# Attention of the sample sequences: GpSimd issues the odd fills, ScalarE copies the odd chunks of turned keys

## What is computed

```python
def gathered_attention(q, t, kg, vg, s, tbl):
    logits = jnp.einsum('bqgrd,bqgnd->bqgrn', q, kg, ...) * (q.shape[-1] ** -0.5)
    ...
    p = masked_softmax(logits + ..., ...)
    return jnp.einsum('bqgrn,bqgnd->bqgrd', p.astype(vg.dtype), vg)
...
o_slc = gathered_attention(qa, t, gather_rows(c_slc_k, page_table, ks, s, g_a), gather_rows(c_slc_v, page_table, vs, s, g_a), s, tbl_a)
o_win, _ = dense_attention(qa, t, k_w, v_w, s_w, tbl_a, WINDOW)
o_b = gathered_attention(qb, t, k_b, v_b, s_b, tbl_b)
```

## Time and profile before

| | us |
|---|---|
| median of 3 runs | 3385.72 |
| lowest and highest of them | 3378.32 and 3390.58 |
| the profiled execution's own time | 3371.94 |
| its span | 3370.3 |
| TensorE busy in the span | 2977.2 (88%) |
| VectorE busy | 1373.4 (41%) |
| ScalarE busy | 708.3 (21%) |
| GpSimd busy | 108.4 (3%) |

### The profile page before, as it was taken

How to read it: one execution, slowest core, us unless ns; L and a number is a source line. 1 busy time by engine, 2 the same in 40 slices (tenths; PEclk the granted TensorE clock), 3 DMA queues, 4 the chain that set the end, 5 groups by cost and what they waited for, 6 DMA issues and landing times. The chain is left out here.

```text
span 3370.3 us, 56792 instructions
## 1 busy us (share of the span) xinstructions
PE 2977.2 (88%) x22144; PEld 2631.9 (78%) x22144; DVE 1373.4 (41%) x2245; ACT 708.3 (21%) x1084; POOL 108.4 (3%) x150
## 2 busy tenths in 40 slices
PE   6799999999975889897887775599799999999897
PEld 3599999999963478786553554499699999999897
DVE  2322222212214368465741666633533343333433
ACT  2211111211102021120000443321322222222222
POOL 0000000000000000000000112100000000000000
PEclk8799999999987899897986887799899999999998
DMA  9765676777544732333897223343233333334331
GB/s 342 229 188 168 196 219 209 224 220 218 172 130 125 209 117 61 108 100 96 276 303 248 79 95 129 111 131 87 66 95 104 94 93 92 104 93 114 108 89 51
DMA packets 594867, 496.75 MB, mean 147 GB/s; under 512 B 37148, under 2 KB 515885, under 8 KB 593885
## 3 DMA queue, kind: packets, MB, share of 16 engines
q1 hardware_dynamic: 528408, 408.45, 41.3%
q10 hardware_dynamic: 58496, 60.59, 5.5%
q0 software_dynamic: 7840, 26.10, 2.0%
HBM read 460.02 MB, written 48.70 MB: 151 GB/s over the span
## 5 line engine op out<-in xcount | busy, mean ns | idle before, releaser
L146 PE MATMUL psum<-h_high,w_high 128*128 128x260 f32 x4992 | 1009.3, 283 | 21.6 <-DVE w_low L133 21.6
L146 PE MATMUL psum<-h_high,w_low 128*128 128x260 f32 x4992 | 1006.9, 283 | 0.0
L146 PE MATMUL psum<-h_low,w_high 128*128 128x260 f32 x4992 | 1005.2, 283 | 0.0
L146 PEld LDWEIGHTS psum<-h_high,w_high 128*128 128x128 f32 x4992 | 770.5, 189 | 35.9 <-issue 30.1
L146 PEld LDWEIGHTS psum<-h_high,w_low 128*128 128x128 f32 x4992 | 770.7, 189 | 0.0
L146 PEld LDWEIGHTS psum<-h_low,w_high 128*128 128x128 f32 x4992 | 768.9, 189 | 0.0
L133 DVE TENSOR_TENSOR w_low<-w,w_high 128x2048 fp32r<-128x2048 f32 x162 | 370.9, 2291 | 591.6 <-ACT w_high L128 591.6
L128 ACT ACTIVATE w_high<-w 128x2048 fp32r<-128x2048 f32 x162 | 309.2, 1910 | 479.5 <-PE psum L146 361.3
L609 DVE COPY pj_out<-psum 128x260 f32<-128x260 f32 x66 | 28.3, 429 | 429.8 <-PE psum L146 429.8
L567 ACT ACTIVATE pj_out<-psum 128x260 f32<-128x260 f32 x66 | 25.6, 388 | 593.9 <-PE psum L146 593.9
L199 PE MATMUL psum<-w,c 128*32 128x512 f32 x768 | 105.3, 661 | 26.1 <-DMA w<-in_w_ada 17.5
(11 more groups left out here) (374 smaller groups left out, 2829.2 us busy)
## 6 DMA issues: line engine op xcount, KB each, us to landing
w<-in_w_ada SPq DMA_DIRECT2D x96, 1024.0 KB, 8.1
w<-in_w_in_att SPq DMA_DIRECT2D x65, 1024.0 KB, 11.7
w<-in_w_in_conv SPq DMA_DIRECT2D x64, 1024.0 KB, 6.3
proj<-pj_out POOLq DMA_DIRECT2D x66, 260.0 KB, 5.0
cz_pgk<-in_cache_nsa_cmp_k SPq DMA_DIRECT2D x128, 128.0 KB, 2.1
cz_pgv<-in_cache_nsa_cmp_v SPq DMA_DIRECT2D x128, 128.0 KB, 2.2
w<-in_w_out_att SPq DMA_DIRECT2D x16, 1024.0 KB, 6.4
w<-in_w_out_conv SPq DMA_DIRECT2D x16, 1024.0 KB, 6.3
```

Of the source, the lines that this page charges most:

```text
L146: mm = pe.matmul(k.psum[:, banks + hf, 0:HC], w[:, kt, :], x[:, kt, hf * HC:(hf + 1) * HC], start=(kt == 0 and m == 0), stop=(kt == KT - 1 ...
```

## The change

SP keeps the even fills. The odd fills go from ScalarE to GpSimd, which issues fills 1, 3, 5 and 7 ahead of its memsets and the others behind them. The copies of turned keys are split by the chunk's number: VectorE copies the even chunks (bank 3), ScalarE the odd ones (bank 4), and the one semaphore `kept` becomes two, `kept_v` and `kept_a`. ScalarE's exponentials now stand between its copies. The odd slots' arrival semaphores are allocated once for the program instead of in the stage.

```diff
+    arrived = [k.at_filled[b // 2] if b % 2 else k.sem(f"at_arrived{b}") for b in range(SLOTS)]
...
+        def keep_keys(eng, kind, s):
+            tb, u, odd = INFO[kind][1] // 2, KINDS.index(kind) * NS + s, int(eng is nc.scalar)
+            if u >= 2:
+                eng.wait_ge(used, u - 1)
+            for c in range(odd, tb, 2):
+                q = chunk0[kind] + s * tb + c
+                to, turned_keys = kt[:, s % 2, :, c * 256:(c + 1) * 256], ps[:, 3 + q % 2, :].rearrange("p (g q) -> p g q", g=G)
+                eng.wait_ge(turned, q + 1)
+                if odd:
+                    eng.activation(to, turned_keys, ACT.Copy).then_inc(kept_a, 1)
+                else:
+                    eng.tensor_copy(to, turned_keys).then_inc(kept_v, 1)
...
             @block.gpsimd
             def _(pool):
+                for n in range(1, SLOTS, 2):
+                    fill(pool, n)
                 pool.memset(pns[:, :, :], 0.0).then_inc(padded, 1)
                 pool.memset(pts_all[:, :, :, :], 0.0).then_inc(padded, 1)
                 pool.memset(pts_win[:, :, :, :], 0.0).then_inc(padded, 1)
                 pool.wait_ge(padded, 3)
+                for n in range(SLOTS + 1, len(fills), 2):
+                    fill(pool, n)
...
-                            pe.wait_ge(kept, q - 1)
+                            pe.wait_ge(kept_a if q % 2 else kept_v, q // 2)
...
-                    pe.wait_ge(kept, chunk0[kind] + (s + 1) * (npg // 2))
+                    for kept in (kept_a, kept_v):
+                        pe.wait_ge(kept, (chunk0[kind] + (s + 1) * (npg // 2)) // 2)
...
-                after = {fill_of["dsa", 0, 5] + 6: "slc", fill_of["slc", 1, 3] + 6: "dsa", fill_of["dsa", 1, 3] + 6: "win"}
-                for n in range(1, len(fills), 2):
-                    fill(act, n)
...
+                for s in range(NS):
+                    keep_keys(act, "slc", s)
+                for s in range(NS):
+                    keep_keys(act, "dsa", s)
+                    if s == 2:
+                        exponentials("slc")
+                exponentials("dsa")
+                for s in range(NS):
+                    keep_keys(act, "win", s)
+                exponentials("win")
```

More of the change, by code:

```diff
@@ L1209, in stage_attend_samples @@
             "dsa": (1, PG, "cache_dsa_k", "cache_dsa_v", KB, "dsa_v_s", None)}
-    vnew_in, turned, kept, used, padded, vused, o_kept, o_turned, added = (
-        k.sem("at_" + n) for n in ("vnew", "turned", "kept", "used", "padded", "vused", "o_kept", "o_turned", "added"))
+    vnew_in, turned, kept_a, kept_v, used, padded, vused, o_kept, o_turned, added = (
+        k.sem("at_" + n) for n in ("vnew", "turned", "kept_a", "kept_v", "used", "padded", "vused", "o_kept", "o_turned", "added"))
     top, maxed, top_all, shifted, topped, exped, summed, sum_all, rated, prob, diag, pt_mm, placed = (
@@ L1217, in stage_attend_samples @@
     SLOTS = 8
-    arrived = [k.sem(f"at_arrived{b}") for b in range(SLOTS)]
+    arrived = [k.at_filled[b // 2] if b % 2 else k.sem(f"at_arrived{b}") for b in range(SLOTS)]
     fills = [(kind, kv, f) for kind, kv in PHASES for f in range(NS * INFO[kind][1] // 8)]
@@ L1517, in exponentials @@
                         nc.scalar.activation(pn[:, i, sh:sh + 1], ps[0:32, MISC[kind], sh:sh + 1], ACT.Exp, bias=st[0:32, i, 1, sh:sh + 1]).then_inc(exped[kind], 1)
-                after = {fill_of["dsa", 0, 5] + 6: "slc", fill_of["slc", 1, 3] + 6: "dsa", fill_of["dsa", 1, 3] + 6: "win"}
-                for n in range(1, len(fills), 2):
-                    fill(act, n)
[L1523 to L1530, removed]
+                act.wait_ge(cs_step, 3)
+                nc.scalar.activation(cs_p[:, 0, :], ps[0:NS * NH, 3, 0:NCB], ACT.Exp, bias=cs_st[:, 1:2], accum_out=cs_st[:, 2:3]).then_inc(cs_exp, 1)
+                act.wait_ge(cs_out, 1)
+                nc.scalar.activation(cs_pt[:, :], ps[:, 3, 0:NS * NH], ACT.Copy).then_inc(cs_kept, 1)
+                for s in range(NS):
[8 more added lines that the diff above has]
+                exponentials("win")
             @block.vector
@@ L1573, in compressed @@
                         dve.tensor_copy(cols(k.oS[:, 0, :]), cols(ps[:, 4 - g, 256:256 + R])).then_inc(cs_step, 1)
[L1575 to L1583, removed]
                 def own_tops(kind):
@@ L1670, in _ @@
                 for s in range(NS):
-                    keep_keys("slc", s)
+                    keep_keys(dve, "slc", s)
                 for s in range(NS):
-                    keep_keys("dsa", s)
+                    keep_keys(dve, "dsa", s)
                     if s == 0:
@@ L1689, in _ @@
                 for s in range(NS):
-                    keep_keys("win", s)
+                    keep_keys(dve, "win", s)
                 keep_outs("dsa", "win")
@@ L2436, in build @@
         k.y_out = [k.sem(f"y_out{b}") for b in range(2)]
+        k.at_filled = [k.sem(f"at_filled{b}") for b in range(4)]
         k.w_in = [k.sem(f"w_in{s}") for s in range(4)]
```

## The result

The changed kernel takes 3388.17 us (median of 12 runs, 3382.39 to 3391.50) against 3380.19 us of the kernel before on the same chip (12 runs, 3374.29 to 3390.58). The ratio is 1.0021, with a 95% interval of 1.0012 to 1.0031: slower by 4 to 10 us. That lies inside the 0.3% that the forecast called no change and is still a loss that can be measured; the forecast had no term for it. The profiled execution took 3385.51 us, its span is 3383.8.

A forecast was written before the change was run, and what follows sets the result against it. Key part bound by the copy-transpose ring, coinciding with VectorE's limit; value part by transfers. Terms sum to -0.3 us on 3371.94, so 3371.6; the runs' median lies 13.8 higher, hence 3385. Own range 3377 to 3395; 8-in-10 range 3374 to 3425.

The forecast's parts named there:

- Ring: Key part: copy and transposes take turns on each PSUM bank, 1.44 us a pair; splitting copies gains only at sequence starts, -1 us.
- GpSimd's issue: Page fills: GpSimd issues 264 more DMAs at 0.67 us each, a fill in 5.9 us; it fits barely, adding 0.
- the first rival: Page fills: GpSimd's issue is serial or slower in a row; stage ends 35 to 114 us later; chance 0.24.
- Exponentials: Key part: an odd key copy on ScalarE waits behind exponentials until 1681.89, once; +0.7 us.
- ScalarE's lost issues: Page fills: ScalarE no longer issues the odd fills; its queue waited for slots, so this is worth nothing.
- Moved memsets: Stage start: GpSimd's memsets end at about 1599, the value part needs them after 1720; no effect.
- Half the bytes on another queue: Value part: odd fills move to GpSimd's queue, no difference in cost per byte taken; 0, ends 6 us either way.
- The sum: Changed stage: all terms together, -1 + 0.7 + 0 + 0 = -0.3 us, on the profiled execution's 3371.94.

## Why the prediction was wrong, point by point

- **Ring, right.** Pairs turn in 1.45 us. ScalarE's copy is 0.597 us, not 0.69, and shortens only its own bank. A sequence gained 0.17 us where under 0.1 was forecast; the key part gained 1.4 us (115.8 against the mean of 116.8 and 117.7), for -1 forecast.
- **GpSimd's issue, right.** 0.58 us for 0.67 taken, with pauses of 2.7 and 3.0 us between fills in the key part: no wait for GpSimd's issue was added, and the first rival, with a chance of 0.24, fell. A pace of 1 us is not to be seen.
- **Exponentials, +0.7: too much.** The odd copy behind them starts at 1679.00 in the changed kernel, 1.17 us behind the even one instead of the usual 0.43, as forecast; but that sequence takes 7.68 us instead of 7.33, so +0.35 reaches TensorE's pace. ScalarE's lost issues, 0: no run told them apart from the ring.
- **Moved memsets, "Nothing": wrong.** I asked what waits for the memsets and not what stands beside them. The lead got 1.8 us shorter (29.6 against 31.4), half of what a second profile of before varies by itself.
- **"Half the bytes on another queue": the step that failed.** The forecast put this term at 0, with ends of 6 us either way for what a byte costs on each queue; that cost stayed (347 GB/s against 348). The value part measured +6.5 us, and from which fill gets the bytes first: SyncE's fill 66 came 6.5 us later into the part, behind GpSimd's 67. The forecast's held the clue, as the packets are larger on one queue: 26.10 MB in 7840 packets against 60.59 MB in 58496.
- **No term for other stages.** The sum ended with the changed stage. That put the second prompt stage at nothing without a reason; it lost 6.1 us, through the stores that GpSimd issues there. The Trainium skill, "SBUF — State Buffer", section "Who interferes with whom", describes ports that GpSimd shares with VectorE in its two-port modes: whoever issues first has them for the whole instruction, and the other stands still. The 2.14 us, which end behind GpSimd's instruction, agree; the 0.52 us in the same order before do not.
- **The sum.** Between the first profiles, lead, key part, value part and prompt 2 give -1.8 - 0.9 + 6.5 + 6.1 = +9.9 us, inside the measured 4 to 10; these executions lie 13.5 us apart, 4.0 of them in the first prompt stage, which varies by as much in kernels with no fill on GpSimd. That the forecast's 3385 came within 3 us of 3388.17 is luck: it stands on three runs of before with a median of 3385.72, and twelve have 3380.19. On that scale the forecast is 3380.

## What to carry to other kernels

Where two queues feed one consumer in turn, equal total rate is not enough: compare the bytes per packet and the order in which fills land, and look for the last wait that everything behind it hangs on. Queues with equal packets kept the order here; a hold on one of them mended 3.7 of 6.5 us. Before work is put beside GpSimd or taken from there, list VectorE's instructions with both ends in SBUF in every stage that GpSimd issues or computes in: here some stood still for up to 1.6 us beside a store and 4.4 us beside memsets. And when a measured loss is larger than the changed stage's, cut both traces at the same landmarks before looking for a cause.

## What the runs showed of the hardware

- In some stretches two queues got equal counts of packets (553 and 551, 1330 and 1310), so bytes went there by packet size: 78% to GpSimd's packets of 3.4 KB on average. From 1800 to 1807 us the counts were 526 and 1095, and GpSimd's queue still got 59% of the bytes.
- The same 1 KB rows went in packets of 4096 bytes when GpSimd issued the fill and of 1024 bytes when SyncE or ScalarE did.
- GpSimd's transfers in a row are issued every 0.58 us.
- VectorE's 128x512 product in SBUF, started 0.30 us into GpSimd's issue of a store, took 0.52, 1.25, 1.24 and 2.12 us with 74 to 79 transfers issued by GpSimd before, and 2.12 to 2.15 us as soon as 8 more had gone ahead, some 500 us earlier. Why 8 transfers matter so long after was not found. The long ones end 0.28 us behind GpSimd's next instruction.
- Two table copies of 32x64 took 4.69 us beside GpSimd's memsets and 0.28 us alone.
